# Differential attention's scores as one product over 96 stacked rows of high and low parts

## What is computed

```
q = rope(q.reshape(B, S, 4, 2, 32)); k = rope(k.reshape(B, S, 4, 2, 32))   # two maps per head
s = einsum('bhmqd,bhmkd->bhmqk', q_block, k) * 32 ** -0.5                  # contraction over 32
p = masked_softmax(s, causal)
a = p[map 0] - lam * p[map 1]
o = rmsnorm(a @ v) * (1 - lam_init)
```

## Time and profile before

| | |
|---|---|
| runs | 2712.06, 2712.3, 2714.15 us |
| the profiled execution's own time | 2713.11 us |
| its span, first to last instruction | 2711.8 us |
| granted TensorE clock, mean over the span | 0.997 of full speed |
| TensorE busy | 2672.0 us of the span |
| VectorE, ScalarE busy | 1630.6 and 1023.0 us |
| mixer of layer 0, first to last score matmul | 1062.4 to 1127.1 us |
| mixer of layer 1, the same | 2093.9 to 2158.5 us |

### The profile page before, as it was taken

How to read it: one execution, slowest core, us unless ns; L and a number is a source line. 1 busy time by engine, 2 the same in 40 slices (tenths; PEclk the granted TensorE clock), 3 DMA queues, 4 the chain that set the end, 5 groups by cost and what they waited for, 6 DMA issues and landing times.

```text
span 2711.8 us, 35115 instructions
## 1 busy us (share of the span) xinstructions
PE 2672.0 (99%) x14437; PEld 2197.6 (81%) x14437; DVE 1630.6 (60%) x3267; ACT 1023.0 (38%) x1757; POOL 14.1 (1%) x43
## 2 busy tenths in 40 slices
PE   8999999999999999999999999999999999999999
PEld 5788888889888888666888889888889666888888
DVE  7766555356767556687776746763346777633334
ACT  4642332435222234565422224322234565422223
POOL 1000000000000000000000000000000000000000
PEclk9999999999999999999999999999999999999999
DMA  8255433133655334411555524543224421233331
GB/s 253 91 173 168 113 95 117 63 109 109 216 187 187 109 103 121 128 32 32 186 186 186 186 90 144 187 142 106 94 90 121 126 63 32 69 103 93 99 99 67
DMA packets 345352, 330.56 MB, mean 122 GB/s; under 512 B 13410, under 2 KB 334694, under 8 KB 345192
## 3 DMA queue, kind: packets, MB, share of 16 engines
q1 hardware_dynamic: 344820, 327.77, 38.8%
q10 hardware_dynamic: 372, 0.55, 0.1%
HBM read 319.89 MB, written 2.10 MB: 119 GB/s over the span
## 4 chain that ended last, share of the span: by engine, by line
PE 93%; DVE 5%; ACT 1%; DMA 0%; SPq 0%; issue 0%; DVEq 0%
PE bank L537 26%; PE bank L539 26%; PE bank L538 26%; PE bank L591 3%; PE bank L2408 1%; PE bank L2437 1%; PE bank L565 1%; PE bank L566 1%; PE bank L567 1%; DVE w_lo L505 1%; PE bank L1395 1%; PE bank L2049 1%; PE bank L1385 1%; DMA mw<-in_w_mod 0%; DVE E L2532 0%; PE bank L874 0%
## 5 line engine op out<-in xcount | busy, mean ns | idle before, releaser
L537 PE MATMUL bank<-h_lo,w_hi 128*128 128x512 f32 (+1 forms) x2432 | 917.4, 377 | 3.6 <-DVE h_lo L716 2.2
L539 PE MATMUL bank<-h_hi,w_lo 128*128 128x512 f32 (+1 forms) x2432 | 894.4, 368 | 0.0
L538 PE MATMUL bank<-h_hi,w_hi 128*128 128x512 f32 (+1 forms) x2432 | 892.6, 367 | 0.0
L505 DVE TENSOR_TENSOR w_lo<-raw,w_hi 128x1024 fp32r<-128x1024 f32 (+1 forms) x420 | 488.9, 1200 | 324.6 <-ACT w_hi L499 324.5
L499 ACT ACTIVATE w_hi<-raw 128x1024 fp32r<-128x1024 f32 (+1 forms) x420 | 419.7, 1035 | 345.9 <-PE bank L539 327.9
L537 PEld LDWEIGHTS bank<-h_lo,w_hi 128*128 128x128 f32 x2432 | 458.3, 188 | 87.0 <-issue 8.2
L538 PEld LDWEIGHTS bank<-h_hi,w_hi 128*128 128x128 f32 x2432 | 458.8, 189 | 76.2 <-issue 4.8
L539 PEld LDWEIGHTS bank<-h_hi,w_lo 128*128 128x128 f32 x2432 | 457.7, 188 | 77.1
L537 PE MATMUL bank<-a_lo,w_hi 128*128 128x512 f32 (+1 forms) x1056 | 391.0, 370 | 0.0
L539 PE MATMUL bank<-a_hi,w_lo 128*128 128x512 f32 (+1 forms) x1056 | 384.7, 364 | 0.0
L538 PE MATMUL bank<-a_hi,w_hi 128*128 128x512 f32 (+1 forms) x1056 | 384.1, 364 | 0.0
(11 more groups left out here) (319 smaller groups left out, 2560.8 us busy)
## 6 DMA issues: line engine op xcount, KB each, us to landing
swf<-in_w_ada SPq DMA_DIRECT2D x60, 1024.0 KB, 8.0
raw<-in_ffn_w_gate SPq DMA_DIRECT2D x44, 1024.0 KB, 5.4
raw<-in_ffn_w_up SPq DMA_DIRECT2D x44, 1024.0 KB, 5.4
raw<-in_w_in SPq DMA_DIRECT2D x40, 1024.0 KB, 5.1
raw<-in_ffn_w_down SPq DMA_DIRECT2D x32, 1024.0 KB, 5.1
raw<-in_w_in SPq DMA_DIRECT2D x32, 512.0 KB, 5.1
raw<-in_ffn_w_down SPq DMA_DIRECT2D x16, 768.0 KB, 4.6
mw<-in_w_mod SPq DMA_DIRECT2D x8, 1024.0 KB, 11.8
```

The costliest lines, as they stand in the source:

```text
L505: nc.vector.tensor_tensor(o, r, half(w_his[place_of[i]], i, h)[0].bitcast(F32), ALU.subtract).then_inc(*w_lo.up((i, h)))
L537: nc.tensor.matmul(o, w1, al, start=start, stop=False)
L538: nc.tensor.matmul(o, w1, ah, start=False, stop=False)
L539: return nc.tensor.matmul(o, w2, ah, start=False, stop=stop)
```

## The change

Per layer and per rope piece (renumbered: 0 is dq tile 0, 1 is dk tile 0, 2 is dq tile 1, 3 is dk tile 1):

- The rope's sum stays in `tmp`. ScalarE makes its high part (`act_high`) and VectorE its low part (`dve_low_part`) in `d_hl`.
- SyncE writes both parts (512 KB) to a buffer in device memory (`sp_parts`), waits for it to land, and reads it back with three transfers of 256 KB (`sp_stack`) into a stack of 96 partitions: 32 rows high, 32 low, 32 high for the queries; high, high, low for the keys. In the stack the four pairs of head and map lie side by side along the row.
- A score matmul is one `float32r` product over 96 partitions, which gives high x high + low x high + high x low in one.
- The score steps of tile c wait for stack transfers 2c and 2c + 1.
- The order in the programs of ScalarE, VectorE and SyncE at the mixer's start is rewritten: ScalarE's four rope copies go first, the `act_high` calls lie between `act_xa`, `act_w` and `act_dv`, and `act_high` 3 stands ahead of `act_dv` 1 to 3; SyncE's order is rope 0, rope 1, parts 0, rope 2, stack 0, parts 1, a weight load, stack 1, rope 3, a weight load, parts 2, parts 3, stack 2, stack 3, rope 4.

```diff
@@ -328,8 +328,8 @@
     def carve(start):
         place = [start]
 
-        def here(name, cols):
-            t = sb(name, cols, at=place[0])
+        def here(name, cols, dt=F32):
+            t = sb(name, cols, dt, at=place[0])
             place[0] += (cols * 4 + 63) // 64 * 64
             return t
 
@@ -390,9 +390,11 @@
     gmu = sb("gmu", 1024, at=at_a + 16384)
     gx = sb("gx", 1024, at=at_a + 16384)
     dat = sb("dat", 1024, at=at_a + 4096)
-    dq = sb("dq", 1024, at=at_a + 16384 + 4096)
-    dk = sb("dk", 1024, at=at_a + 8192)
-    swaps = [sb(f"swap{i}", 512, at=at_a + 16384 * i + 12288) for i in range(2)]
+    d_hl = [sb(f"d_hl{i}", 1024, F32R, at=at_a + (8192, 16384 + 4096)[i]) for i in range(2)]
+    swaps = [sb("swap0", 512, at=at_a + 12288), here("swap1", 512)]
+    QS = [sb("QS0", 2048, F32R, at=at_swf), here("QS1", 2048, F32R)]
+    KS = [sb("KS0", 2048, F32R, at=at_swf - 8192), sb("KS1", 2048, F32R, at=at_a + 16384 + 8192)]
+    parts = [nc.dram_tensor(f"parts{p}", [128, 1024], F32, kind="Internal").ap() for p in range(4)]
 
 
     groups = vector_rows(A)
@@ -1980,34 +1982,29 @@
     ld_ws, ld_bs = sig("ws_in"), sig("bs_in")
     swap_in = [sig(f"swap{i}_in") for i in range(2)]
     cross_in = [sig(f"cross{i}_in") for i in range(2)]
-
-    PAIR = {("dq", 0): 0, ("dq", 1): 1, ("dk", 0): 2, ("dk", 1): 3, ("n0", 0): 4, ("n0", 1): 5, ("n1", 0): 6,
+    parts_out = [sig(f"parts{p}_out") for p in range(4)]
+    stack_in = [sig(f"stack{p}_in") for p in range(4)]
+
+    PAIR = {("dq", 0): 0, ("dk", 0): 1, ("dq", 1): 2, ("dk", 1): 3, ("n0", 0): 4, ("n0", 1): 5, ("n1", 0): 6,
             ("n1", 1): 7, ("kk", 0): 8, ("kk", 1): 9}
 
     def pair(p):
+        if p in (2, 3):
+            return (tmp[4], tmp[5]) if p == 2 else (tmp[6], exs[0])
         return tmp[p % 2 * 2], tmp[p % 2 * 2 + 1]
 
     def rope_where(l, p):
 
         if p < 4:
-            t = dat[:, 0:512], dat[:, 512:1024]
-        else:
-            t = NC_, NS_
-        every = slice(0, 128)
-        if p < 2:
-            d = [(every, dq[:, p * 512:p * 512 + 512])]
-        elif p < 4:
-            d = [(every, dk[:, (p - 2) * 512:(p - 2) * 512 + 512])]
-        elif p < 8:
-            d = [(every, nq[:, (p - 4) * 512:(p - 4) * 512 + 512])]
-        else:
-            d = [(every, (ks, kw)[p - 8][:, 0:512])]
-        return t, d
+            return (dat[:, 0:512], dat[:, 512:1024]), pair(p)[1][:, :]
+        if p < 8:
+            return (NC_, NS_), nq[:, (p - 4) * 512:(p - 4) * 512 + 512]
+        return (NC_, NS_), (ks, kw)[p - 8][:, 0:512]
 
     def act_rope(l, key, p):
         act.wait_ge(pe, key)
-        if p >= 2:
-            act.wait_ge(dve, ("rd", l, p - 2))
+        if p >= 4:
+            act.wait_ge(dve, ("rd", l, p - 2 if p >= 6 else p - 4))
         nc.scalar.activation(pair(p)[0][:, :], ps.of(key)[:, :], ACT.Copy).then_inc(*act.up(("rq", l, p), lets=key))
 
 
@@ -2019,7 +2016,7 @@
             nc.sync.dma_start(swaps[p % 2][r:r + n, :], pair(p)[0][o:o + n, :]).then_inc(*swap_in[p % 2].up((l, p), 16))
 
     def dve_rope(l, p):
-        (cos, sin), dsts = rope_where(l, p)
+        (cos, sin), d = rope_where(l, p)
         q0, q1 = pair(p)
         dve.wait_ge(ld_da if p < 4 else ld_l2, l)
         dve.wait_ge(act, ("rq", l, p))
@@ -2028,9 +2025,32 @@
         dve.wait_ge(swap_in[p % 2], (l, p))
         nc.vector.tensor_tensor(q0[:, :], q0[:, :], sin, ALU.mult).then_inc(*dve.up(("rs", l, p)))
         dve.wait_ge(dve, PREV)
-        for i, (r, d) in enumerate(dsts):
-            nc.vector.tensor_tensor(d, q0[r, :], q1[r, :], ALU.add).then_inc(
-                *dve.up(("rd", l, p) if i == len(dsts) - 1 else ("rd", l, p, i)))
+        nc.vector.tensor_tensor(d, q0[:, :], q1[:, :], ALU.add).then_inc(*dve.up(("rx" if p < 4 else "rd", l, p)))
+
+    def act_high(l, p):
+        if p >= 2:
+            act.wait_ge(parts_out[p - 2], l)
+        act.wait_ge(dve, ("rx", l, p))
+        nc.scalar.activation(d_hl[p % 2][:, 0:512], pair(p)[1][:, :], ACT.Copy).then_inc(*act.up(("rh", l, p)))
+
+    def dve_low_part(l, p):
+        if p >= 2:
+            dve.wait_ge(parts_out[p - 2], l)
+        dve.wait_ge(act, ("rh", l, p))
+        nc.vector.tensor_tensor(d_hl[p % 2][:, 512:1024], pair(p)[1][:, :], d_hl[p % 2][:, 0:512].bitcast(F32),
+                                ALU.subtract).then_inc(*dve.up(("rd", l, p)))
+
+    def sp_parts(l, p):
+        sp.wait_ge(dve, ("rd", l, p))
+        nc.sync.dma_start(parts[p], d_hl[p % 2][:, :].bitcast(F32)).then_inc(*parts_out[p].up(l, 16))
+
+    def sp_stack(l, p):
+        st, order = ((QS, (0, 1, 0)), (KS, (0, 0, 1)))[p % 2]
+        src = parts[p].rearrange("(j p) (a s) -> a p j s", j=4, a=2)
+        sp.wait_ge(parts_out[p], l)
+        for i, a in enumerate(order):
+            nc.sync.dma_start(st[p // 2][32 * i:32 * i + 32, :].bitcast(F32).rearrange("p (j s) -> p j s", j=4),
+                              src[a]).then_inc(*stack_in[p].up(l, 16))
 
 
     DSC, NSC = 32.0 ** -0.5, 0.125
@@ -2044,10 +2064,11 @@
                 w = (b + 1) * 128
                 for m in range(2):
                     t = bank(("ds", l, s, m), M_SC)
-                    pe.wait_ge(dve, ("rd", l, 3))
-                    r = slice((par * 2 + m) * 32, (par * 2 + m) * 32 + 32)
-                    nc.tensor.matmul(t[:, 0:w], dq[r, c * 512 + b * 128:c * 512 + b * 128 + 128],
-                                     dk[r, c * 512:c * 512 + w], start=True, stop=True).then_inc(*pe.up(("ds", l, s, m)))
+                    pe.wait_ge(stack_in[2 * c], l)
+                    pe.wait_ge(stack_in[2 * c + 1], l)
+                    o = (par * 2 + m) * 512
+                    nc.tensor.matmul(t[:, 0:w], QS[c][0:96, o + b * 128:o + b * 128 + 128], KS[c][0:96, o:o + w],
+                                     start=True, stop=True).then_inc(*pe.up(("ds", l, s, m)))
             n = s - 5
             if 0 <= n < 16 and n % 2 == 0:
                 c, b, _ = DA_ITEMS[n]
@@ -2090,6 +2111,7 @@
         if not 0 <= n < 16 or da_copier(l, n)[0] is not e:
             return
         w = (DA_ITEMS[n][1] + 1) * 128
+        e.wait_ge(dve, ("rd", l, 3))
         e.wait_ge(pe, ("dt", l, n))
         if n >= 4:
             e.wait_ge(pe, ("dav", l, (n - 4) // 2 * 2 + 1))
@@ -2779,14 +2801,20 @@
         nc.scalar.activation(lv[:, 2:4], lv[:, 0:2], use(ACT.Exp)).then_inc(*act.up(("l2", l)))
         act_w(("dk", l))
         act_rope(l, ("dq", l, 0), 0)
-        act_rope(l, ("dq", l, 1), 1)
+        act_rope(l, ("dq", l, 1), 2)
+        act_rope(l, ("dk", l, 0), 1)
+        act_rope(l, ("dk", l, 1), 3)
         act_w(("xa", l))
+        act_high(l, 0)
         act_xa(l, 0)
-        act_rope(l, ("dk", l, 0), 2)
+        act_high(l, 1)
         act_xa(l, 1)
-        act_rope(l, ("dk", l, 1), 3)
+        act_w(("dv", l), 1, 0)
+        act_high(l, 2)
         act_w(("dv", l))
-        for tb in range(4):
+        act_dv(l, 0)
+        act_high(l, 3)
+        for tb in range(1, 4):
             act_dv(l, tb)
         da = act_da(l)
 
@@ -2885,11 +2913,20 @@
         nc.vector.tensor_scalar(lv[:, 6:7], lv[:, 4:5], -1.0, None, ALU.mult).then_inc(*dve.up(("l6", l)))
         dve_w(("xa", l))
         dve_rope(l, 0)
+        dve_low_part(l, 0)
         dve_rope(l, 1)
+        dve_low_part(l, 1)
+        dve_w(("dv", l), 1, 0)
+        dve_rope(l, 2)
         dve_w(("dv", l))
-        dve_rope(l, 2)
+        dve_low_part(l, 2)
+        gx0 = dve_gx(l, 0)
+        next(gx0)
         dve_rope(l, 3)
-        for _ in dve_gx(l, 0):
+        next(gx0)
+        next(gx0)
+        dve_low_part(l, 3)
+        for _ in gx0:
             pass
         dve_gates(l)
         da = dve_da(l)
@@ -2965,6 +3002,7 @@
         b4 = ("f", l, 0)
         if plan[b4]:
             pool.wait_ge(dve, ("acc", ada_end[b4]))
+        pool.wait_ge(pe, ("ds", l, 7, 1))
         nc.gpsimd.memset(kcz[:, :], 0.0).then_inc(*pool.up(("zn", l)))
         pool.wait_ge(ld_ws, l)
         w4 = tmp[2][:, :].rearrange("p (g s) -> p g s", g=4)
@@ -2992,9 +3030,25 @@
         for m in range(2):
             nc.sync.dma_start(w2_of(m), A["nsa_cmp_w2_2"][l, m].rearrange("(c p) n -> p c n", p=128)).then_inc(
                 *ld_w2.up(l, 16))
-        swap_after = {("dk", l): (0, 1), ("xa", l): (2, 3), ("nq", l, 0): (4, 5), ("nq", l, 1): (6, 7), ("kk", l): (8, 9)}
-        for n in names[index["dk", l]:index["vv", l]]:
+        sp_raw(index["dk", l] + 2)
+        sp_rope(l, 0)
+        sp_rope(l, 1)
+        sp_raw(index["xa", l] + 2)
+        sp_parts(l, 0)
+        sp_rope(l, 2)
+        sp_stack(l, 0)
+        sp_parts(l, 1)
+        sp_raw(index["dv", l] + 2)
+        sp_stack(l, 1)
+        sp_rope(l, 3)
+        swap_after = {("nq", l, 0): (4, 5), ("nq", l, 1): (6, 7), ("kk", l): (8, 9)}
+        for n in names[index["nq", l, 0]:index["vv", l]]:
             sp_raw(index[n] + 2)
+            if n == ("nq", l, 0):
+                for p in (2, 3):
+                    sp_parts(l, p)
```

(2 more changed lines are left out.)

## The result

The changed kernel takes 2734.6 us (median of 6 runs, 2733.2 to 2738.3) against 2712.2 us (6 runs, 2711.8 to 2714.2): ratio 1.008, 95% interval 1.007 to 1.009. It is 22.4 us slower. Forecast were 2734.3 us and a range of 2724 to 2748. The profiled execution took 2734.62 us, span 2733.3 us, granted clock 0.991 (before 0.997).

A forecast was written before the change was run, and what follows sets the result against it. TensorE was taken as the bound. Per layer, 11.0 us late start plus 3.3 low clock minus 3.3 saving gave 11.0, so 22.0 in all: 2735.1 us against the profiled execution, 2734.3 as median; range 2724 to 2748.

The forecast's parts named there:

- The mechanism: In `dv`: block 3 waits for `act_dv` 1, queued behind `act_high` 3 and late swaps; TensorE waits some 8 to 9 us.
- No rival: Clock holds 2727.7 us (0.14); transfers longer 2742.5 (0.20); stack saves nothing 2740.9 (0.05); waits stay hidden 2705.7 (0.05).
- The start of block 3: TensorE starts `dv` block 3 at 1067.5 instead of about 1056.5: 11.0 us late per layer.
- the mis-sized term: SyncE's parts 1, before stack 1: landing 3.6 us after issue, taken from a 512 KB load of the same size.
- the high bound: Upper bound on parts 1's landing time: 6.1 us, from a weight load of 1024 KB.
- The slow-transfer rival: Parts 1 take 6.1 us and the last swap 3.6: 4.1 us more per layer, 2742.5 us; chance 0.20.
- The low clock: TensorE slower after the wait ahead of `dv` block 3: 3.3 us lost per layer, bounds 0 and 3.4.
- The saving: Score product: 7.4 us less TensorE time per layer, of which 3.3 us reach the end, between 0 and 5.
- Steps 0 to 7: Score steps where TensorE sets the pace: 2.4 of 3.7 us saved arrive, because VectorE's work comes in bunches.
- Steps 8 to 14: Score steps where VectorE sets the pace: the other 3.7 us only lengthen TensorE's idle time, except in the last step.
- The last step and what follows it: Last score step, run at the low clock and taking 1.83 us: about 0.9 us saved.
- The sum: Per layer 11.0 + 3.3 - 3.3 = 11.0 us slower, 22.0 us for both layers.

The follow-up runs named there:

- experiment 1: Changed kernel with `act_high` 3 moved behind `act_dv` 3 in ScalarE's program, nothing else different: 2720.4 us, ratio 1.0031.
- experiment 5: Changed kernel with one 1 MB weight load issued behind rope 3 instead of between parts 1 and stack 1: 2731.5 us, ratio 1.0071.
- experiment 8: Changed kernel with the same transfers and product, but the orders on ScalarE, VectorE and SyncE rewritten, including parts 1 ahead of stack 0: 2711.8 us, ratio 0.9996.
- experiment 2: Changed kernel with 34 extra 512-column matmuls, never read, between `dv` blocks 2 and 3 to keep TensorE busy: 2732.8 us, ratio 1.0071.
- experiment 4: Kernel before with only the score product changed to single-pass over 96 rows of `dq` and `dk`, no parts or stacks: 2705.2 us, ratio 0.9972.
- experiment 7: Changed kernel with parts and stacks kept, but scores computed in float32 on 32 rows of the stacks: 2742.5 us, ratio 1.0112.
- experiment 3: Changed kernel with SyncE's rope 3 issued ahead of stack 1 instead of behind it: 2728.0 us, ratio 1.0054.

## Why the prediction was right, and where its terms were not

**The mechanism** was as put. TensorE waits ahead of `dv` blocks 2 and 3 (1.94 and 8.47 us; 2 to 3 and 8 to 9 forecast), ScalarE is idle ahead of its last high part (12.4 us, longer than the 8 to 9 forecast), the clock is near 0.5 behind, and experiment 1 removes the long wait by moving one line. No rival happened as such.

**The start of block 3** was forecast 11.0 us late; it is 12.4: the row of before below (TensorE in order of time, block 3's first matmul) against 1070.93 - 2.06 = 1068.87.

```profile
1056.49 0.29 PE L580 MATMUL bank<-w_hi,h_lo 128*128 128x280 f32 x1
```

Link by link, net of 2.06 us: parts 0 were issued at 1044.2 (forecast 1044.4); swaps cost 0.70 us each, as put; an issue of a stack 0.42 to 0.52 instead of 0.6, one of parts 0.35 to 0.43. So parts 1 went out at 1051.9, 0.5 us early. Then the mis-sized term: 5.45 us to landing in place of 3.6. It was priced by an equal transfer alone in its queue, and experiments 5 and 8 show that the neighbour which matters is not the weight load that I had for the high bound, but stack 0's three reads ahead of it. The last swap took 2.6 instead of 2.0 us. The slow-transfer rival had the right direction; a third of its 4.1 us came.

**The low clock** was put at 3.3 us per layer, by the loss behind the earlier trace rows. It is 2.05: TensorE is 12.4 us late at block 3's start, 14.4 to 14.5 at its end, and experiment 2 has 12.4 at that end. The 7 us of low clock in the earlier trace rows were taken over as they stood. There the clock is 0.50 from 1126.2 to 1133.1, all of it behind the wait and filled with work. Here it falls while TensorE still stands, and only 4.4 of its 10.2 us (1065.1 to 1075.4) cost anything. The forecast had no term for the low clock of block 2, and none was needed, since block 3 waits anyway.

**The saving** was put at 3.3 us per layer and is 4.8: 14.4 - 9.6. Experiments 4 and 7 give 7.9 us for both layers at the end, 4 each. Steps 0 to 7 brought 14.4 - 11.0 = 3.4 us instead of 2.4; I had discounted for bunches of VectorE's work, and nearly all of the 3.7 arrived. Steps 8 to 14 brought next to nothing, as said: the wait ahead of the last step grew from 3.44 to 4.32 us (forecast 2 to 4 more, so too much). The last step and what follows it brought 1.4 instead of 0.9; about 1 us of that, by estimate, is because the low clock begins at 1136.8, 2.1 us ahead of the step, while before it begins at 1126.2, 0.3 us behind the step's start.

**The sum** per layer is 12.4 + 2.05 - 4.8 = 9.6 instead of 11.0. The median came out 0.3 us from the forecast, which is partly luck: 19.4 us are in the layers, 22.4 in the medians. In the two profiled executions 2.06 us stand in the stretch ahead of the layers, and the profiles of this study scatter there by as much; whether anything of the 3.0 us outside the layers belongs to the change stays open.

**The rule on array packing.** The Trainium skill (TensorEngine Tiling (Array Packing), Overview) allows a packed contraction of 32 rows up to four times the speed. In the runs the packed float32 pair of maps costs 1.15 us at 512 columns, and the two 96-row single-pass matmuls 0.70 - 0.23 = 0.47 us. The measurement decides: giving up the packing together with float32 lost nothing here. That float32 costs more than the packing gives is an inference; no run has the float32 product without the packing, or the single-pass product with it.

## What to carry to other kernels

Price a changed operand path by the order of the queues that it passes through: with the same product and the same transfers the kernel is 22 us slower or 3 us faster than before, depending on the order of the instructions on SyncE, ScalarE and VectorE. In an in-order program, a copy that frees a bank for the bottleneck engine does not belong behind an operation that waits for a transfer. And a landing time read from a transfer that is alone holds only where nothing large was issued just ahead of it on the same queue.

## What the runs showed of the hardware that was not expected

- The landing of a small transfer depends on its predecessors. The `swap` transfers (32 and 64 KB) land in 2.0 us as a median of the changed kernel, with a maximum of 5.5 (3.6 before); in experiment 3, behind 1.5 MB in the same queue, even the last one of 32 KB took over 5.5 us. All swaps of the changed kernel:

```profile
DMA to landing us min/median/max: 1.9/2.0/5.5
```

- 512 KB to device memory lands in at most 3.2 us with little ahead of it (experiment 8) and in 5.45 behind three transfers of 256 KB. Parts 0 of the changed kernel, 1.8 us behind a weight load of 1 MB, took 5.3: a load ahead delays a transfer too, the load of experiment 5 did not because it stood behind.
- The low clock behind TensorE's wait of 8.5 us costs 2.05 us, and the one behind its wait of 1.9 us in experiment 1 costs 1.6; keeping TensorE busy through the long wait brought 1.8 us of both layers' 4.1 to the end.
- The stretch from the start to the first 70 us differs by up to 2.2 us between executions of kernels that are equal there, which is as much as several of the effects studied; differences inside a layer must be taken from instructions, not from the span.
